# Two expert layers of a decoder trunk: interleaved expert products against two passes with DRAM scratch

## The reference

```python
x = x + stick_breaking_attention(rmsnorm(x), w_qkv, w_o)          # layer 0
x = x + peer_ffn(rmsnorm(x), w_q0, keys_1, keys_2, u0, v0)
x = x + mla_attention(rmsnorm(x), ...)                            # layer 1
x = x + peer_ffn(rmsnorm(x), w_q1, keys_1, keys_2, u1, v1)
return rmsnorm(x, final_norm_g)

def peer_ffn(h, ...):            # h: 256 tokens x 2048; u, v: 16384 experts x 2048
    ids, g = two_level_top_k(h)                  # 8 heads x 16 experts a token, softmax g
    act = gelu(einsum('ced,cd->ce', u[ids], h))
    return einsum('ce,ced->cd', g * act, v[ids])
```

## Time and profile before

| | |
|---|---|
| runs | 4446.27 us median of 3 (4444.6 to 4454.43) |
| span of the profiled execution | 4447.9 us |
| PE busy / DVE busy / ACT busy / POOL busy | 94% / 72% / 38% / 24% |
| DMA engines busy (main queue) | 41.2% |

### The profile page before, as it was taken

The page is one execution under the profiler, slowest core; times in us unless marked ns, Lnnn a source line. Parts: engine busy times, 40 slices in busy tenths (PEclk is TensorE's granted clock), DMA queues, the critical chain, the costliest instruction groups (busy, mean ns, idle before and its releaser), DMA issues.

```text
span 4447.9 us, 62861 instructions
## 1 busy us (share of the span) xinstructions
PE 4182.9 (94%) x23214; PEld 3505.8 (79%) x23214; DVE 3196.6 (72%) x4459; ACT 1682.2 (38%) x1996; POOL 1057.3 (24%) x442
## 2 busy tenths in 40 slices
PE   7997899999999999999988998899999999999998
PEld 6876777888888888888777677788888888888877
DVE  4444598877877777787646548987877787787775
ACT  3344432333333333333343342333333333333333
POOL 1223354211111111111111024432222222222221
PEclk9998999999999999999988899999999999999999
DMA  4441443444444444444433143344444444444444
GB/s 179 181 169 56 154 160 124 171 161 161 170 165 161 167 170 160 164 171 161 170 133 142 49 164 139 123 156 158 171 166 157 170 170 154 170 170 161 161 161 151
DMA packets 94853, 689.62 MB, mean 155 GB/s; under 512 B 10896, under 2 KB 10896, under 8 KB 10896
## 3 DMA queue, kind: packets, MB, share of 16 engines
q1 hardware_dynamic: 94176, 682.73, 41.2%
q10 hardware_dynamic: 432, 3.15, 0.2%
HBM read 683.73 MB, written 2.10 MB: 154 GB/s over the span
## 4 chain that ended last, share of the span: by engine, by line
PE 87%; DVE 7%; issue 4%; ACT 1%; POOL 0%; DMA 0%; DVEq 0%; SPq 0%; ACTq 0%; POOLq 0%
PE bank L1210 25%; PE bank L1230 14%; PE bank L1231 13%; PE bank L1232 13%; PE bank L1209 12%; PE bank L1308 6%; DVE lo L663 1%; PE bank L1212 1%; DVE match L803 1%; PE bank L1246 1%; DVE act_t L689 0%; PE bank L1271 0%; POOL st_a L419 0%; ACT act_t L486 0%; PE bank L1273 0%
## 5 line engine op out<-in xcount | busy, mean ns | idle before, releaser
L457 ACT ACTIVATE hi<-raw 128x1024 fp32r<-128x1024 f32 x1294 | 1370.2, 1060 | 2266.7 <-PE bank L1232 1114.3
L1210 PE MATMUL bank<-act_t,hi 128*128 128x512 f32 x5120 | 1859.4, 407 | 78.0 <-issue 54.7
L401 POOL TENSOR_TENSOR lo<-raw,hi 128x1024 fp32r<-128x1024 f32 x395 | 1016.0, 2573 | 3316.9 <-ACT hi L457 3316.9
L663 DVE TENSOR_TENSOR lo<-raw,hi 128x1024 fp32r<-128x1024 f32 x899 | 1113.3, 1239 | 921.2 <-ACT hi L457 916.1
L1209 PE MATMUL bank<-act_t,lo 128*128 128x256 f32 x4800 | 1371.7, 286 | 0.0
L1210 PEld LDWEIGHTS bank<-act_t,hi 128*128 128x128 f32 x5120 | 980.0, 194 | 292.0 <-issue 59.6
L1209 PEld LDWEIGHTS bank<-act_t,lo 128*128 128x128 f32 x4800 | 934.0, 195 | 15.2
L1230 PE MATMUL bank<-hi,wa 128*128 128x512 f32 x2048 | 820.6, 401 | 7.8 <-DVE wa L891 7.8
L1232 PE MATMUL bank<-hi,wa 128*128 128x512 f32 x2048 | 810.7, 396 | 0.0
L1231 PE MATMUL bank<-lo,wa 128*128 128x512 f32 x2048 | 810.6, 396 | 0.0
L1230 PEld LDWEIGHTS bank<-hi,wa 128*128 128x128 f32 x2048 | 388.1, 190 | 96.9 <-DVE wa L891 8.1
(11 more groups left out here) (206 smaller groups left out, 2617.1 us busy)
## 6 DMA issues: line engine op xcount, KB each, us to landing
raw<-in_stream SPq DMA_DIRECT2D x647, 1024.0 KB, 4.8
x_res<-in_x SPq DMA_DIRECT2D x2, 1024.0 KB, 6.0
keys_sb<-in_keys ACTq DMA_DIRECT2D x2, 1024.0 KB, 4.8
out<-xn SPq DMA_DIRECT2D x2, 1024.0 KB, 4.0
gain_row<-in_final_g ACTq DMA_DIRECT2D x1, 1024.0 KB, 4.3
gain_t<-in_gains SPq DMA_DIRECT2D x1, 44.0 KB, 1.7
pos_i<-in_positions SPq DMA_DIRECT2D x1, 1.0 KB, 6.9
invf<-in_inv_freq SPq DMA_DIRECT2D x1, 16.0 KB, 8.8
```

Of the source, the lines that this page charges most:

```text
L401: pool.tensor_tensor(lo[:, s, :], raw[:, n0 % RAW_SLOTS, j * HALF:(j + 1) * HALF], hi[:, s, :].bitcast(F32), ALU.subtract).then_inc(lo_rea ...
L457: act.activation(hi[:, s, :], raw[:, slot, j * HALF:(j + 1) * HALF], ACT.Copy).then_inc(hi_ready[s], 1)
L663: dve.tensor_tensor(lo[:, s, :], raw[:, n0 % RAW_SLOTS, j * HALF:(j + 1) * HALF], hi[:, s, :].bitcast(F32), ALU.subtract).then_inc(lo_read ...
L1210: ins = mm(ps[:], w_hi, act_t[:, kt, :, :].rearrange("p w t -> p (w t)"), start=first, stop=last)
```

## The change

The expert layer becomes two passes: first all 128 u units, then all 128 v units, one v unit now being one tile by all 2048 output columns. No engine has a loop any more, every instruction is written out.

- **Pass 1.** Gelu'd tiles go through a ring of 8 tiles, and each group of four is stored in DRAM (`store_acts`, 0.5 MB).
- **Routing weights once.** 32 batches a layer instead of 128: a batch is 8 tokens by all 128 tiles. `one_hots` is 24 tensor_scalar instructions of 128 float16 elements with one or two per-partition scalars; `build_w` is 16 matmuls of 128 columns; ACT moves them from PSUM to a 32 KB buffer (`stage_weights`, two instructions), and SP stores 32 pieces a layer of 0.5 MB, in runs of 256 bytes (`store_weights`).
- **Where a batch stands.** Batch b belongs to tile 10 + 3b: DVE makes the one-hots at the end of that tile's turn, behind `sum_tile`; PE multiplies them in the middle of the next unit; ACT stages them in the turn after.
- **Pass 2.** The output of both token halves stays in all eight banks from the first to the last v unit; `x_res` is added to once. Activations and weights of a group come back from DRAM (`load_group`), two groups ahead; one multiplication for each group (`weigh`).

```diff
-BATCH = 16
-BODY_BATCHES = 4
-AHEAD = 5
-UNROLL = 3
+BATCH = 8
+BATCHES = S // BATCH
+BATCH_TILE = 10
+BATCH_STEP = 3
+FLUSH = 8
+PIECES = 8
+STAGED = 2 * GROUP
+SP_LEAD = 6
...
+def batch_at(tile):
+    b, off = divmod(tile - BATCH_TILE, BATCH_STEP)
+    return b if off == 0 and 0 <= b < BATCHES else None
...
+            def store_weights(layer, f, piece):
+                sp.wait_ge(w_free, layer * BATCHES + FLUSH * (f + 1))
+                at, i = FLUSH_TOK * f, PIECE * piece
+                sp.dma_start(w_dram[layer][i:i + PIECE, :, at:at + FLUSH_TOK].rearrange("i p t -> p i t"),
+                             w_stage[f % 2][:, i:i + PIECE, :]).then_inc(w_stored[f % 2], 16)
...
+            def peer(layer):
+                base = U0[f"peer{layer}"]
+                for n in range(2 * TILES):
+                    done = n - SP_LEAD
+                    g, at = divmod(done, GROUP)
+                    if 1 <= g <= GROUPS and at == 0:
+                        store_acts(layer, g - 1)
+                    f, at = divmod(done - BATCH_TILE - 4, BATCH_STEP * FLUSH)
+                    piece, odd = divmod(at, 2 if f < FLUSHES else 1)
+                    if 1 <= f <= FLUSHES and piece < PIECES and odd == 0:
+                        store_weights(layer, f - 1, piece)
...
+                    if g + 2 < GROUPS and g >= 0 and at == 0:
+                        load_group(layer, g + 2)
+                    load(base + n)
...
+                def stage_weights(b):
+                    act.wait_ge(w_full, layer * BATCHES + b + 1)
...
+                    for r in range(2):
+                        ins = act.activation(
+                            w_stage[f % 2][:, :, tok + 4 * r:tok + 4 * (r + 1)].rearrange("p i t -> p t i"),
+                            ps_w[b % 2][r][:].rearrange("p (t i) -> p t i", i=NKEYS), ACT.Copy, scale=1 / WEIGHT_SCALE)
+                    ins.then_inc(w_free, 1)
...
+                def one_hots(b):
-                    dve.tensor_tensor(hot2[:, b % 2, :, :], iota_rep[:],
-                                      i2_t[:, bass.ds(tok, BATCH)].unsqueeze(1).to_broadcast([P, P, BATCH]),
-                                      ALU.is_equal)
...
+                    for t in range(BATCH):
+                        tok = BATCH * b + t
+                        dve.tensor_scalar(hot2[:, b % 2, t, :], iota[:], sel_t[:, 1, tok:tok + 1], None, ALU.is_equal)
+                        for w in range(2):
+                            ins = dve.tensor_scalar(hot1g[:, b % 2, t, w, :], iota[:], sel_t[:, 0, tok:tok + 1],
+                                                    sel_t[:, 2 + w, tok:tok + 1], ALU.is_equal, ALU.mult)
+                    ins.then_inc(hots_ready, 1)
+                def weigh(g):
+                    dve.wait_ge(aw_in[g % 2], 32 * (layer * (GROUPS // 2) + g // 2 + 1))
+                    dve.tensor_tensor(acts[g % 2][:], acts[g % 2][:], w_part[g % 2][:], ALU.mult).then_inc(weighted, 1)
...
@@ vector: peer @@
+                for j in range(TILES):
                     split_lo(base + j + LEAD)
...
+                    sum_tile(j)
...
+                    if batch_at(j) is not None:
+                        one_hots(batch_at(j))
+                    if j >= TILES - GROUP:
+                        prepare(j - TILES)
+                for t in range(TILES):
+                    split_lo(out0 + t + LEAD)
+                    prepare(t)
+                for q in range(QUARTERS):
...
+                    for c in range(NC_TOK):
+                        r = x_res[:, c, 512 * q:512 * (q + 1)]
+                        dve.tensor_tensor(r, r, ps_out[c][q][:], ALU.add).then_inc(v_added, 1)
...
+                def build_w(b):
                     pe.wait_ge(hots_ready, layer * BATCHES + b + 1)
...
                     for t in range(BATCH):
-                        ins = mm(ps_c[(c0 + b) % 2][:, t * 2 * WQ_TILES:(t + 1) * 2 * WQ_TILES],
-                                 hot2[:, b % 2, :, t], hot1g[:, b % 2, :, :, t].rearrange("p w i -> p (w i)"),
-                                 start=True, stop=True)
+                        o = ps_w[b % 2][t // 4][:, (t % 4) * NKEYS:(t % 4 + 1) * NKEYS]
+                        mm(o, hot2[:, b % 2, t, :], hot1g[:, b % 2, t, 0, :], start=True, stop=False)
+                        ins = mm(o, hot2[:, b % 2, t, :], hot1g[:, b % 2, t, 1, :], start=False, stop=True)
...
+                def out_unit(t):
+                    g, i = divmod(t, GROUP)
+                    if i == 0:
+                        pe.wait_ge(wa_lo, layer * GROUPS + g + 1)
+                    for j, s, k in halves(out0 + t):
+                        pe.wait_ge(lo_ready[s], k + 1)
+                        for c in range(NC_TOK):
...
+                            a_hi, a_lo = (wa[g % 2][:, i, w, c * P:(c + 1) * P] for w in range(2))
+                            cols = [(ps_out[c][2 * j + q], slice(512 * q, 512 * (q + 1))) for q in range(2)]
+                            for o, at in cols:
+                                mm(o[:], a_hi, hi[:, s, at], start=first, stop=False)
+                            for o, at in cols:
+                                mm(o[:], a_hi, lo[:, s, at], start=False, stop=False)
+                            for o, at in cols:
+                                ins = mm(o[:], a_lo, hi[:, s, at], start=False, stop=last)
+                        ins.then_inc(used[s], 1)
...
@@ tensor: peer @@
+                for j in range(TILES):
+                    b = batch_at(j - 1)
...
+                        unit_a(base + j, a0 + j, middle=(lambda b=b: build_w(b)) if b is not None else None)
+                pe.wait_ge(w_free, (layer + 1) * BATCHES)
+                for t in range(TILES):
+                    out_unit(t)
```

More of the change, by code:

```diff
@@ L317, in build_program, with halves, unit_done @@
         GRANTED = 2
-        def halves(n0, it, per):
+        def halves(n0):
             for j in range(2):
                 h = 2 * n0 + j
-                yield j, h % HALF_SLOTS, plus(h // HALF_SLOTS, it, 2 * per // HALF_SLOTS)
+                yield j, h % HALF_SLOTS, h // HALF_SLOTS
         def gpsimd_takes(n0, s):
-            busy = any(U0[f"wq{k}"] + LEAD <= n0 < U0[f"peer{k}"] + AHEAD_TILES + LEAD for k in range(2))
+            busy = any(U0[f"wq{k}"] + LEAD <= n0 < U0[f"peer{k}"] + TURN_TILE + 3 + LEAD for k in range(2))
             return s >= 1 if busy else s == HALF_SLOTS - 1
[L330 to L336, removed]
+        def unit_done(engine, n0):
+            *_, (_, s, k) = halves(n0)
             engine.wait_ge(used[s], k + 1)
@@ L358, in _, with store_acts @@
[L358 to L364, removed]
+                sp.dma_start(raw[:, slot, :], stream[n0]).then_inc(raw_in[slot], 16)
+            def store_acts(layer, g):
+                sp.wait_ge(gelu_done, layer * TILES + GROUP * (g + 1))
+                at = GROUP * (g % 2)
+                sp.dma_start(a_dram[layer][g], stage[:, at:at + GROUP, :].rearrange("p h t -> p (h t)")).then_inc(
+                    a_stored[g % 2], 16)
@@ L365, in _ @@
+            for n in range(U0["peer0"]):
                 load(n)
+            peer(0)
+            for n in range(U0["c"], U0["peer1"]):
+                load(n)
+            peer(1)
             for c in range(NC_TOK):
@@ L404, in split_range @@
             def split_range(first, last):
[L405 to L413, removed]
+                for n in range(first, last):
+                    split_lo(n)
             def mask_head(h, src, dst, ring, ready, freed, done):
@@ L452, in split_hi @@
                 slot = n0 % RAW_SLOTS
-                act.wait_ge(raw_in[slot], plus(16 * (n0 // RAW_SLOTS + 1), it, 16 * per // RAW_SLOTS))
-                for j, s, k in halves(n0, it, per):
-                    if it is not None or k > 0:
+                act.wait_ge(raw_in[slot], 16 * (n0 // RAW_SLOTS + 1))
+                for j, s, k in halves(n0):
+                    if k > 0:
                         act.wait_ge(used[s], k)
@@ L460, in split_range @@
             def split_range(first, last):
[L461 to L469, removed]
+                for n in range(first, last):
+                    split_hi(n)
             def root_mean_square(k, rows, junk, width, col):
@@ L494, in squares @@
                 act.wait_ge(b_free, GRANTED + b_first + q + 1)
[L495 to L498, removed]
+                square_block(q)
             def x_norm():
@@ L526, in peer @@
             def peer(layer):
[L527 to L532, removed]
-                    act.activation(st, st, ACT.Gelu).then_inc(gelu_done, 1)
[L535 to L539, removed]
+                base, out0 = U0[f"peer{layer}"], U0[f"peer{layer}"] + TILES
@@ L541, in peer, with coefficients_hi @@
+                def coefficients_hi(g):
+                    act.wait_ge(weighted, layer * GROUPS + g + 1)
+                    if g >= 2:
+                        unit_done(act, out0 + GROUP * (g - 1) - 1)
```

(35 more changed lines are left out.)

349 lines of the change are left out of this document (114 added, 235 removed).

## The result

The changed kernel takes 4780.8 us (median of 4 runs, 4779.4 to 4784.2) against 4446.9 us of the kernel before on the same chip: ratio 1.0754, 95% interval 1.0738 to 1.0769. It is slower, as forecast, but by 334 us where 119 were forecast, and it lies above the range.

The account below looks back on a forecast made before the run. The prediction took PE's own work and its waits to bound the kernel: 4447.9 - 211 (one-hot products) - 102 (loops) - 12 (old waits) + 442 (batch waits) + 3 (end) = 4568, forecast as 4565 us, range 4350 to 4660.

Parts of the forecast that it names:

- Pass 2 and the end: Second pass and final adds: coefficients come two groups ahead; later `x_res` adds and copies cost 3 us for two layers.
- pass 2 at 1.00 without a wait: Expected sign: the second pass runs at granted clock 1.00, PE never waiting, 717 us a layer.
- The batch wait: PE waits in pass 1 for DVE's one-hots: 4.9 us plus 2.0 of lost clock, 64 batches, 442 us.
- the lower bound: Cheapest batch waits: 3.8 and 1.65 us, no lock, clock lost only behind the longer, 238 us in all.
- The lock: DVE's one-hots and POOL's half exclude each other, taken as true: 2.4 us more in every second batch.
- Rival 1: DVE and POOL work side by side during the one-hots: 77 us less, 4490 us; chance 0.20.
- Rival 2: Short one-hots on DVE, 0.15 us each, and no lock: faster, 4364 us; chance 0.20.
- Rival 3: Weight stores in 256-byte runs fill the DMA queues: 4615 us at 8 us a store; chance 0.07.
- Rival 4: Gains and losses cancel, a batch costing within 0.3 us of 5.0: 4437 to 4455 us; chance 0.03.
- The loops: PE's 18 loop boundaries go when unrolled: 62 us of waiting and 40 us of half clock, 102 us saved.
- The one-hot products: On PE, 64 batches of 16 matmuls replace 256, at 1.1 us each: 211 us saved.
- their old waits: PE's four waits for one-hots in the kernel before, 8.0 us, 12 with the clock, go.

Follow-up runs that it names:

- experiment 2: Changed kernel with only the lo part of the coefficients moved ahead of the split in a group's last unit: 4567.4 us, ratio 1.0276.
- experiment 6: Changed kernel with 20 unused products of 512 columns on PE ahead of each wait for the one-hots: 4652.9 us, ratio 1.0468.
- experiment 7: Changed kernel with the coefficients' lo ahead of the split, and PE's one-hot products and ACT's staging two units later: 4131.6 us, ratio 0.9297.
- experiment 9: Changed kernel with coefficients' lo ahead of the split, PE's one-hot products two units later, one-hots in two parts behind neighbouring tiles: 4105.7 us, ratio 0.9235.
- experiment 5: Changed kernel with 16 one-hot operations a batch instead of 24, PE's 16 products kept: 4707.6 us, ratio 1.0592.
- experiment 1: Changed kernel with PE's one-hot products and ACT's staging one unit later: 4395.7 us, ratio 0.9892.
- the fastest version: The kernel of experiment 9: 4105.7 us, ratio 0.9235.
- experiment 4: The kernel before with every engine loop written out, nothing else: 4358.1 us, ratio 0.9806.

## Why the prediction was wrong, point by point

**The step that failed** is "*Pass 2 and the end.* Coefficients come two groups ahead", and with it "pass 2 at 1.00 without a wait, 128 x 5.6 = 717 us a layer". The loads of a group are issued two groups ahead. But I looked at the transfers and not at the last operation before PE, the lo of the coefficients on DVE, and didn't ask behind which wait it stands. It was the same question that I had asked of the one-hots, and the same unit's end that answers it. The term measured 213 us (experiment 2) where the sum had none; 141 us are the waits (134.9 and 6.1, the first group of each layer), and most of the rest is the clock behind them, which fell in layer 1 (0.93) and not in layer 0 (1.00). With it the sum is 4568 + 213 = 4781 us; 4780.8 were measured. The agreement to the microsecond is chance, as the other terms' errors cancel.

**The batch wait** was right in mechanism and size. Forecast 4.9 us a batch, seen 5.1 (324.0 / 64); clock forecast 2.0, seen 2.0 (experiment 6). That makes 452 us against the term's 442. By the repaired versions it lies in the same place: experiment 7 regained 4567.4 - 4131.6 = 436 us over experiment 2, with a part of the waits moved to the sum, and experiment 9, without them, 462. Within it the one-hots took 4.8 us instead of 4.6, and the second scalar cost about 0.06 us (0.22 against 0.16). That the clock's 2.0 would be less behind a shorter wait, as the lower bound had it, is not borne out at 3.3 us (experiment 5); behind 1.6 us the clock stayed at 1.00 (experiment 1).

**The lock** between DVE and POOL is there for these operations too: the 2.38 us row. Rival 1 falls. By the Trainium skill ("SBUF — State Buffer", section "SBUF: two separate sides") the two exclude each other when DVE is in a two-port mode, which tensor_scalar can enter; the trace agrees, with an operation that ended 0.05 us after POOL's 2.40 us; in which mode DVE was, it doesn't show.

**Rival 2** fell with 0.16 and 0.22 us an operation and with the lock. **Rival 3** fell: the DMA share rose to 0.72 in pass 1 of the fastest version and PE waited for none of it. The weights' stores land in 7.5 us (median), against 6.7 us for the equally large stores of activations in 4 KB rows, and where eight of them a layer come one to a unit, neither ACT nor DVE waits for a load. **Rival 4** fell with 7.1 us a batch against its 5.0.

**The loops** were forecast at 102 us and measured at 87 (experiment 4). The profiles split it: PE's idle time fell by 56 us (265.0 to 208.9, span less busy time), where 62 were forecast from 16 waits of 54.7 us in all, scaled up to 18. The clock gave the rest: PE worked at the low clock for 260 us before and for 186 in experiment 4, and half of the difference is 37 us, against 40. The two profiled executions differ by 91 us, the medians by 87.

**The one-hot products** at 211 us and their old waits at 12 have no run of their own. The traces size the first: at full clock a batch of the new ones holds PE for 0.88 us instead of 1.1 (experiment 9, every batch), one of the old for 1.05 (experiment 4, median), so 256 x 1.05 - 64 x 0.88 = 213 us. Both prices were a little high, and that cancels. In the changed kernel the new ones ran at the low clock and start 0.11 us apart (776.17 to 776.28), 1.7 us a batch. The fastest version against experiment 4, which differs from it by everything but the loops, gives 4358.1 - 4105.7 = 252 us, against 211 + 12 - 3 = 220. So some 30 us more came back than these terms have; PE's busy time accounts for 245 us of it (4148.4 to 3903.0), part of that at a clock of 0.974 instead of 0.971. The rest was not split further.

**Two slips in the working** changed nothing: at 1.8 us a batch the one-hot products save 166 us and not 164, and 0.3 us a batch around 5.0 is 19 us to either side and not 9 (rival 4).

## What to carry to other kernels

For every operation that a reordering places behind another on the same engine, find the wait in front of it and ask when that one ends; do it for the last operation before the bottleneck engine in every stage, not just for the stage that looks suspicious. Work made on one engine for another should be at least one full turn ahead of the wait in front of it: here one turn left 64 us of waits and two left none. Two shifted indices and one moved call turned a loss of 7.5% into a gain of 7.0%, and splitting the long piece made it 7.65%. And an idle stretch of the matrix engine costs more than its length: here 5.1 us cost 7.1.

## What the runs showed of the hardware that I had not expected

Matmuls whose results are thrown away made the kernel 128 us faster, since they held the clock at 1.00 (experiment 6). A shorter wait, 3.3 instead of 5.1 us, left the clock low for longer, some 80 us more over the run (experiment 5), while waits of 1.6 us left it at 1.00 (experiment 1). A float16 tensor_scalar of 128 columns costs 0.16 us with one per-partition scalar and 0.22 with two. And 64 stores of 2048 runs of 256 bytes each, next to a stream of 1 MB loads, cost no wait of PE, ACT or DVE for a load in the expert layers.
